# Early expert products in three fp32r passes, their remainders split between VectorE and GpSimd, in a one-layer decoder step

## The reference, cut to what matters

```
def chunk_fn(xc):
    q = (xc @ w_query).astype(jnp.float32).reshape(PEER_CHUNK, PEER_HEADS, D_QUERY)
    s1 = jnp.einsum('chk,nk->chn', q[..., :HALF_Q], k1)
    s2 = jnp.einsum('chk,nk->chn', q[..., HALF_Q:], k2)
    v1, i1 = lax.top_k(s1, PEER_TOPK)
    v2, i2 = lax.top_k(s2, PEER_TOPK)
    cand = (v1[..., :, None] + v2[..., None, :]).reshape(PEER_CHUNK, PEER_HEADS, PEER_TOPK * PEER_TOPK)
    sc, ci = lax.top_k(cand, PEER_TOPK)
    e1 = jnp.take_along_axis(i1, ci // PEER_TOPK, axis=-1)
    e2 = jnp.take_along_axis(i2, ci % PEER_TOPK, axis=-1)
    eid = e1 * N_KEYS + e2
    gate = jax.nn.softmax(sc, axis=-1)
    act = jax.nn.gelu(jnp.einsum('chkd,cd->chk', exp_u[eid], xc, preferred_element_type=jnp.float32))
    out = jnp.einsum('chk,chkd->cd', gate * act, exp_v[eid].astype(jnp.float32))
    return out.astype(xc.dtype)
```

## Time and profile before

| | |
|---|---|
| median of 3 runs | 1710.42 us (1708.64 to 1710.57) |
| the profiled execution, its own time | 1709.66 us |
| its span, first to last instruction | 1707.8 us |
| granted TensorE clock, mean over the span | 0.99 |
| busy: PE, DVE, ACT, POOL | 96%, 77%, 36%, 28% |
| the chain that ended last | PE 78%, DVE 2%, DMA 1%, SP's queue 1% |

### The profile page before, as it was taken

The page is one execution under the profiler, slowest core; times in us unless marked ns, Lnnn a source line. Parts: engine busy times, 40 slices in busy tenths (PEclk is TensorE's granted clock), DMA queues, the critical chain, the costliest instruction groups (busy, mean ns, idle before and its releaser), DMA issues.

```text
span 1707.8 us, 24171 instructions
## 1 busy us (share of the span) xinstructions
PE 1645.9 (96%) x8587; PEld 1373.7 (80%) x8587; DVE 1316.1 (77%) x2697; ACT 618.3 (36%) x1034; POOL 484.3 (28%) x511
## 2 busy tenths in 40 slices
PE   7998988999999999987999999999999999999998
PEld 6777664467777669976999999999999999998886
DVE  5788463247898879976888788888888888889976
ACT  5322452221111158862333333333333333333434
POOL 1000000011223300013444444444444444445420
PEclk9999999999999999998999999999999999999999
DMA  8312813032221127888999999999999999999883
GB/s 283 121 69 71 312 66 118 0 140 75 75 74 50 62 80 221 255 269 298 339 349 353 331 347 356 336 338 357 339 337 352 351 336 342 361 336 356 329 313 140
DMA packets 164427, 411.53 MB, mean 241 GB/s; under 512 B 15503, under 2 KB 76461, under 8 KB 162893
## 3 DMA queue, kind: packets, MB, share of 16 engines
q1 hardware_dynamic: 118229, 242.20, 41.2%
q0 software_dynamic: 46080, 167.79, 26.6%
HBM read 375.34 MB, written 33.24 MB: 239 GB/s over the span
## 4 chain that ended last, share of the span: by engine, by line
PE 78%; DVE 2%; DMA 1%; SPq 1%; ACT 1%; issue 0%; DVEq 0%; ACTq 0%
PE bank L1471 30%; PE bank L1423 25%; PE bank L1410 7%; PE bank L1362 7%; PE bank L1340 3%; PE bank L1452 3%; PE bank L1399 1%; DVE placed L1934 1%; DMA u<-in_uT 1%; SPq L1285 1%; DMA gates_kept<-staged 1%; DVE hot_b L1927 0%; DVE here L1930 0%; DVE h_low L1911 0%; PE bank L1332 0%; ACT qh L1525 0%
## 5 line engine op out<-in xcount | busy, mean ns | idle before, releaser
L1471 PE MATMUL bank<-v_parts,p_high 128*128 128x512 f32 x1404 | 434.7, 391 | 2.4 <-DVE p_low L1911 2.4
L1679 POOL DMA_INDIRECT rows<-in_u_rows,row_u x160 | 198.2, 1239 | 399.5 <-DVE dots L1967 219.9
L1471 PEld LDWEIGHTS bank<-v_parts,p_high 128*128 128x128 f32 x1404 | 262.4, 188 | 51.5 <-issue 3.5
L1423 PE MATMUL bank<-h_high,u_high 128*128 128x384 f32 x832 | 282.7, 340 | 10.6 <-DVE u_low L1911 9.9
L1423 PE MATMUL bank<-h_low,u_high 128*128 128x384 f32 x832 | 283.0, 340 | 0.0
L1679 POOL DMA_INDIRECT rows<-in_v,row_u x160 | 212.9, 1331 | 239.4 <-DVE y L1977 170.5
L1423 PE MATMUL bank<-h_high,u_low 128*128 128x384 f32 x832 | 278.7, 335 | 0.0
L1471 PE MATMUL bank<-v_parts,p_low 128*128 128x512 f32 x702 | 273.6, 390 | 0.0
L1911 DVE TENSOR_TENSOR u_low<-u,u_high 128x1024 fp32r<-128x1024 f32 x115 | 140.8, 1224 | 146.7 <-ACT u_high L1560 146.4
L1596 ACT CAST p_high<-gel 128x384 fp32r<-128x384 f32 x128 | 65.8, 514 | 380.6 <-DVE gel L1955 363.5
L1423 PEld LDWEIGHTS bank<-h_high,u_high 128*128 128x128 f32 x832 | 157.0, 189 | 14.8 <-DVE u_low L1911 10.4
(11 more groups left out here) (235 smaller groups left out, 2440.2 us busy)
## 6 DMA issues: line engine op xcount, KB each, us to landing
vv<-in_v SPq DMA_DIRECT2D x117, 512.0 KB, 5.4
u<-in_uT SPq DMA_DIRECT2D x104, 512.0 KB
gate<-gates_kept SPq DMA_DIRECT2D x30, 768.0 KB, 8.3
gates_kept<-staged SPq DMA_DIRECT2D x11, 2048.0 KB, 9.7
early<-in_uT SPq DMA_DIRECT2D x24, 512.0 KB, 3.6
w_in_sb<-in_w_in SPq DMA_DIRECT2D x9, 1024.0 KB, 8.6
wq<-in_w_q SPq DMA_DIRECT2D x16, 512.0 KB, 3.7
ckT<-in_ckT SPq DMA_DIRECT2D x4, 1536.0 KB, 14.5
```

Source lines behind the costliest of these rows:

```text
L1423: ins = pe.matmul(a_ps[par][:, 0:DT], x[:, par, k], y, start=(k == 0 and n == 0), stop=(k == KT - 1 and n == 2))
L1471: ins = pe.matmul(y_ps[2 * (i - 1) + half][:], x[:, b, of], y[:, part], start=(t == 0 and n == 0), stop=(t == NK - 1 and n == 2))
L1679: nc.gpsimd.indirect_dma_start(rows[:, r % ROW_BUFS], None, table, bass.IndirectOffsetOnAxis(ap=row_u[:, s_:s_ + 1], axis=0)).then_inc(fet ...
```

## The change: what it does

1. The 24 early blocks are computed by `activate` too, with three fp32r products instead of one in fp32. `activate_early`, the buffer `early` and its four places are gone; early blocks go through the two places of `u`.
2. ACT rounds them: the two blocks of a head behind the first and the second half of its query copies, the nine others of the last run each behind a gelu. The remainders of blocks 0 to 14 are taken by DVE at the beginning of a head, those of blocks 15 to 23 by POOL: five of them each behind the sums of one tile of head 7, one behind the last, three behind `pick(7)`.
3. `h_high` is rounded and `h_low` taken ahead of head 0 (ACT, POOL). `split_h` is gone from DVE.
4. POOL does `pick(n - 1)` ahead of the sums of head n, no longer behind them.
5. In the 16 x 16 tables of `hits`, `pick` and `decode` the keys are innermost now: the comparison reads the position broadcast along the innermost axis, and the sum reads along it without a stride.
6. The load of block 34 stands between the two last stores.
7. Memory: `h2T` and `h_low` have places of their own; `tops`, `ef`, `gsum`, `shift` and `row_f` lie where `xr` and `g2_row` were.

```diff
-EARLY_BUFS = 4
+BY_POOL = sum(min(n, 2) for n in IN_HEADS.values())
 ...
+        late = Region(nc, base.at + TILES * D * 4, x_region.at)
 ...
-            def load_early(q):
-                wait(sp, a_done, q - EARLY_BUFS + 1)
-                sp.dma_start(early[:, q % EARLY_BUFS], d.uT[q]).then_inc(early_in[q % EARLY_BUFS], 16)
             def load_u(q, par):
-                first = q < WHOLE + 2
-                sp.wait_ge(a_done, q - EARLY_BUFS + 1 if first else q - 1)
+                wait(sp, a_done, q - 1)
 ...
-            for half in range(2):
-                store_last(half)
+            store_last(0)
             load_u(EARLY + 2, EARLY % 2)
+            store_last(1)
 ...
             def activate(q, par, halves=(0, 1)):
                 if 0 in halves:
-                    pe.wait_ge(u_split, q - WHOLE + 1)
+                    if q == 0:
+                        pe.wait_ge(h_split, KT)
+                    if q < 2:
+                        pe.wait_ge(h0s_ready, 2)
+                    if q < BY_POOL:
+                        pe.wait_ge(early_split, q + 1)
+                    elif q < WHOLE:
+                        pe.wait_ge(last_split, q - BY_POOL + 1)
+                    else:
+                        pe.wait_ge(u_split, q - WHOLE + 1)
 ...
+                    for q in early_after(n)[half:half + 1]:
+                        round_u(q, q % 2)
 ...
             act.wait_ge(h_taken, 2 * TILES)
+            for k in range(KT):
+                nc.scalar.copy(h_high[:, k], h2T[:, k, P:END]).then_inc(h_rounded, 1)
             for n in range(PH):
                 head(n)
-                for q in early_after(n)[:7]:
+                for z, q in enumerate(early_after(n)[:9]):
                     gelu(q)
-            for k in range(KT):
-                nc.scalar.copy(h_high[:, k], h2T[:, k, P:END]).then_inc(h_rounded, 1)
+                    for q in early_after(n)[z + 2:z + 3]:
+                        round_u(q, q % 2)
             act.wait_ge(shifted, 2)
 ...
+            for k in range(KT):
+                pool.wait_ge(h_rounded, k + 1)
+                nc.gpsimd.tensor_tensor(h_low[:, k], h2T[:, k, P:END], h_high[:, k].bitcast(F32), ALU.subtract
+                                        ).then_inc(h_split, 1)
+            def split_early(q):
+                pool.wait_ge(u_rounded, q + 1)
+                nc.gpsimd.tensor_tensor(u_low[:, q % 2], u[:, q % 2], u_high[:, q % 2].bitcast(F32), ALU.subtract
+                                        ).then_inc(last_split, 1)
             for n in range(PH):
+                if n:
+                    pick(n - 1)
                 for i in range(tiles_of(n)):
                     sums(n, i)
-                if n:
-                    pick(n - 1)
+                    if n == PH - 1:
+                        split_early(early_after(n)[2 + i])
+            split_early(early_after(PH - 1)[2 + TILES])
             pick(PH - 1)
+            for q in early_after(PH - 1)[3 + TILES:]:
+                split_early(q)
 ...
-                        slot = cab[:, hh, half, i].rearrange("p (o j) -> p o j", o=1)
+                        slot = cab[:, hh, half, i].rearrange("p (j o) -> p j o", o=1)
 ...
-                    nc.vector.tensor_reduce(ef[:, half, 0:m, n], hit[:, half, 0:m].rearrange("p i k j -> p i j k"), AX_X,
+                    nc.vector.tensor_reduce(ef[:, half, 0:m, n], hit[:, half, 0:m], AX_X,
 ...
             def head(n):
                 m = tiles_of(n)
+                for q in early_after(n)[:2]:
+                    low(u_low[:, q % 2], u[:, q % 2], u_high[:, q % 2], u_rounded, q + 1).then_inc(early_split, 1)
 ...
-                if n == HOTS:
-                    dve.wait_ge(a_done, WHOLE)
-                    split_h()
```

More of the change, by code:

```diff
@@ L1099, in route @@
         keysT = sb("keysT", [P, 2, NK])
+        h2T = sb("h2T", [P, KT, T])
         qh = sb("qh", [P, 4, T])
@@ L1113, in route @@
         keyf = sb("keyf", [P, 2, 2, TILES, TOPK])
[L1114 to L1118, removed]
+        tops = late("tops", [P, TILES, PH, TOPK])
+        ef = late("ef", [P, 2, TILES, PH, TOPK])
+        gsum = late("gsum", [P, TILES, PH])
+        shift = late("shift", [P, TILES, PH, TOPK])
+        row_f = late("row_f", [P, FETCHED])
         spreads = sb("spreads", [P, PACK, NS])
@@ L1173, in route @@
         u_rounded, u_split = sem("u_rounded"), sem("u_split")
-        early_in = [sem(f"early_in{b}") for b in range(EARLY_BUFS)]
+        early_split, last_split = sem("early_split"), sem("last_split")
         gates_copied = [sem(f"gates_copied{b}") for b in range(2)]
@@ L1249, in _ @@
             sp.wait_ge(scaled, TILES)
-            for q in range(EARLY_BUFS):
-                load_early(q)
+            for q in range(2):
+                load_u(q, q % 2)
             for n in range(PH):
@@ L1556, in whole @@
                                hot_b[:, n % 2].rearrange("p g k t -> p g t k")).then_inc(hot_made, 1)
-            def round_u(q, par):
-                act.wait_ge(u_in[par], 8 * (q - WHOLE - par) + 16)
-                nc.scalar.copy(u_high[:, par], u[:, par]).then_inc(u_rounded, 1)
-            for q in early_after(PH - 1)[7:-1]:
+            for z, q in enumerate(early_after(PH - 1)[9:-1], 9):
                 gelu(q)
+                for q in early_after(PH - 1)[z + 2:z + 3]:
+                    round_u(q, q % 2)
             whole(0)
@@ L1656, in pick @@
                     for i in range(tiles_of(n)):
-                        key = keyf[:, hh, half, i].rearrange("p (k o) -> p k o", o=1)
+                        key = keyf[:, hh, half, i].rearrange("p (o k) -> p o k", o=1)
                         ins = nc.gpsimd.tensor_tensor(hit[:, half, i], hit[:, half, i],
@@ L1738, in _, with low @@
                 nc.vector.tensor_tensor(h0s[:, half], banks[6 + n][:], g2_row[:, half], ALU.mult).then_inc(h0s_ready, 1)
+            def low(part, whole, high, rounded, value):
+                dve.wait_ge(rounded, value)
+                return nc.vector.tensor_tensor(part, whole, high.bitcast(F32), ALU.subtract)
             def search(n, i):
@@ L1907, in _ @@
             counts = spread(count[:].rearrange("p (o k) t -> p o k t", o=1), [P, TB // 2, NK, 2])
-            def low(part, whole, high, rounded, value):
-                dve.wait_ge(rounded, value)
-                return nc.vector.tensor_tensor(part, whole, high.bitcast(F32), ALU.subtract)
-            def split_h():
-                for k in range(KT):
-                    low(h_low[:, k, P:END], h2T[:, k, P:END], h_high[:, k], h_rounded, k + 1).then_inc(h_split, 1)
             def split_u(q, par):
-                low(u_low[:, par], u[:, par], u_high[:, par], u_rounded, q - WHOLE + 1).then_inc(u_split, 1)
+                low(u_low[:, par], u[:, par], u_high[:, par], u_rounded, q + 1).then_inc(u_split, 1)
             for n in range(BATCHES):
-                if n == HOTS:
-                    dve.wait_ge(a_done, WHOLE)
-                    split_h()
                 if n % (GB // TB) == 2 and n // (GB // TB) in range(1, IN_GATES + 2):
```

35 lines of the change are left out of this document (10 added, 25 removed).

## The result

The changed kernel takes 1720.95 us (median of 4 runs, 1719.27 to 1723.20) against 1710.49 (1708.64 to 1712.12): a ratio of 1.0062, 95% interval 1.0050 to 1.0075. It is 0.6% slower. The forecast was faster, 1703.8, and its range ended at 1711. The profiled execution took 1719.27 us, its span is 1717.2; before it was 1709.66 and 1707.8. So the ledger has to explain 9.4 us of span.

The account below looks back on a forecast made before the run. PE was taken to bound the heads and the steady stage. Terms -12.1 + 8.5 + 5.0 - 2.0 - 6.0 = -6.6 us gave 1703.1 for the profiled execution, a median of 1703.8 us, range 1696.5 to 1711.

Parts of the forecast that it names:

- Heads: Heads 0 to 7: fp32r blocks shorten PE's period from 28.64 to 26.77 us, -12.1 us in all.
- Last run: Blocks 13 to 23: waits for loads, remainders and gates make it 66.5 us instead of 57.96, +8.5, before clock losses.
- that term: PE's clock falling behind gaps in the last run: 3.0 us for the long hole, 2.0 for four others, +5.0.
- POOL's rate: POOL's remainder of 1024 elements: 1.97 us, extrapolated from operations of 56 and 256 elements, bounds 1.6 to 2.5.
- last run at half clock: Rival: blocks from 15 on at 1.2 GHz, about 24 us lost, 1722.8 us; decided at 81.5 us; chance 0.08.
- Start of the gates: After the last run: DVE's remainder of h is gone, so the gates start earlier, -2.0 us.
- Load of block 34: Turn into the steady stage: queued behind one store, not two, the load lands earlier, -6.0 us.

Follow-up runs that it names:

- e6: Changed kernel with POOL's pick behind the sums of a head again, as before; layout and all else kept: 1725.78 us, ratio 1.0090.
- e12: Changed kernel with blocks 13 to 23 as plain fp32 products and the slots innermost again in `hit`: 1697.44 us, ratio 0.9927.
- e5: Changed kernel with the slots innermost again in `hit`, as before the change; all else kept: 1718.21 us, ratio 1.0046.
- e2: Kernel before the change with only the load of block 34 put between the two last stores: 1710.35 us, ratio 0.9999.
- e7: Changed kernel, blocks 13 to 23 plain fp32, loads of u 34, u 35 and v of step 2 between the last store's halves: 1692.44 us, ratio 0.9897.
- e16: e7 plus blocks 13 and 14 as fp32r (1690.43 us), with `h_low` in rows of 544 instead of 384, as before the change: 1688.67 us, ratio 0.9878.

## Why the prediction was wrong

The forecast was a gain, with a chance of 0.08 for slower, and the kernel got slower: two terms were wrong, the last run and the load of block 34.

**Heads: right.** Forecast -12.1, measured -11.4; the heads themselves gave 12.1, and 0.7 is a later start of the first (348.83 for 348.14), which in the profiles of the experiments varies between 347.8 and 350.7. Period 26.68 against 26.77, two blocks 8.52 against 8.40. On DVE the sum takes 1.21 us (I had 1.38 at most). The comparison takes 0.42 undisturbed, just what I took (the mean of 0.44 has some in it that wait for POOL); one starts every 0.34 us instead of 0.20. The casts fell from 0.59 to 0.19, as the move of the pick had suggested, and e6 shows it: without that move heads 4 and 5 are DVE's. In the changed kernel they are at the limit, with periods of 27.02 and 26.82 us. e12 shows that even the old layout fits in.

**Last run: this step failed, by its size.** Forecast 66.5 + 5.0 = 71.5 us; it took 79.8. The mechanism stood in the forecast, gap by gap. By the stretches of PE's products (pairs from block 13 on: 8.61, 10.19, 10.16, 11.22 us; block 21 4.46; the last two 10.42) the 11 blocks took 55.1 us where full clock gives 46. So that term was 9 us, not 5. Against 4.20 us a block the pairs behind the first three gaps lost 1.8, 1.8 and 2.8 us, where I had 2.0 for all gaps, and the two blocks behind the long hole 2.0, where I had 3.0. Not all of it is the clock: the first pair lost 0.2 us and block 21, behind the fourth gap, 0.3 at a granted clock of 1.00, so a start after a wait costs about that by itself, and the clock some 8. The gaps in front of blocks 15, 17, 19 and 21 are 3.11, 3.09, 5.70 and 3.02 us, the hole 8.95 and `turn_slots` 0.9, together 24.8 where I had 20.3. Of these 4.5 us 0.6 in each of three gaps comes mostly from POOL's 2.35 us for a remainder (I took 1.97), and 2.6 from the remainder of block 19; the gap in front of block 21 was 0.6 shorter than forecast and the hole 0.6 longer.

That remainder is the mechanism that I missed. POOL starts it at 591.11. DVE is at its comparisons until 594.10:

```profile
590.67 3.43 DVE L1830 TENSOR_TENSOR hit<-cab,place 128x256 bf16<-128x256 bf16 x10
```

and POOL is done at 596.31, 2.2 us after the last of them, where a whole remainder takes 2.35. The same in the heads: DVE's comparisons run from 440.27, its remainder to 444.17, and POOL's first product ends 0.53 us later.

```profile
441.77 2.93 POOL L1650 TENSOR_TENSOR hit<-hit,keyf 128x256 bf16<-128x256 bf16 x1 [7.53 <-DVE hit L1830]
```

In all six picks of heads 1 to 6 that product ends 0.53 to 0.55 us after DVE's last two-input instruction, whether it took 2.9 or 4.4 us. So there POOL doesn't run slower; it stands still until the run of them ends. By the Trainium skill (SBUF — State Buffer, "Who interferes with whom") "A DVE instruction with two SBUF inputs contends with a GpSimd instruction that reads SBUF", and the one that comes second is blocked. The trace agrees (2.93 us against 0.67), and so do e5 (2.34) and e6 (0.67, picks begun at other times). It doesn't always wait for the whole run, though. In the first pick of head 0 POOL begins in the same way, inside a run of comparisons, and the two take turns, DVE's comparisons at 0.89 us and POOL's products at 0.85; so they do in `pick(7)` of e6. What decides between the two no run shows.

```profile
L1650 POOL TENSOR_TENSOR hit<-hit,keyf x4: 789/850/854, 389.0 to 391.3; 128x256 bf16<-128x256 bf16 x4
```

The change put POOL's first product right beside DVE's longest such run, so that a wait threatens there could have been read from the order beforehand. The page of the Trainium skill that I weighed for POOL's rate (GPSIMD Engine Reference, "3.1 Elementwise — side-by-side cycle accounting") was right as well: the estimate from its 2.6 cycles, with the launch seen here, was 2.4 us, and the remainder takes 2.35 undisturbed. The slope from operations of 56 and 256 elements was a bad basis.

**The rival "last run at half clock"** named 81.5 us as its point of decision. The run ended 1.7 us short of it. It had 0.08. That the time, 1720.95, lies beside its 1722.8 is chance: it wanted half clock in every block from 15 on and 24 us lost by it, and the loss was 9, since part of each pair and all of block 21 ran at full rate. The rest of the way came from longer waits (4.5), the load of block 34 (5.0) and the steady stage (1.9), none of which it had.

**Start of the gates: right**, -1.9 against -2.0.

**Load of block 34: failed.** Forecast -6.0, measured -1.0, and e2 gives 0 on the median (0.9 in its trace). Block 34 did come earlier: 784.28 - 764.32 = 19.96 us after block 32 and not 26.94. The prediction said "The second store and the loads of v behind it come about 2 us later; block 35 then lands just when PE asks for it". The second store landed at 787.45, 23.1 us after block 32 began, where both had landed 20.5 us after it before, and block 35 waited for it by way of v and ACT's queue. I had followed u of 35 to its landing, but not the rounding behind v of step 2. That is also where e7 found the 5 us.

**What was not forecast at all:** 1.9 us in the steady stage, by the layout of `h_low` (e16).

The sum: 0.7 ahead of the heads, 8.3 in the last run, 0.1, 5.0 and 1.9 make the 16 us between -6.6 and +9.4.

## What to carry to other kernels

A cheaper form of a step that needs a longer chain (load, round, split) pays where the chain is hidden, in the heads, and not where the same few buffers are turned over without pause; there one more buffer for the first link brought 14 us and plain fp32 as much. Follow each wait that you remove to the next consumer on every engine's queue, since a transfer or an Exp queued behind the wrong neighbour cost 9 us here and hid a gain of 5. When an edit moves GpSimd's work, look at what VectorE does at that time: a GpSimd instruction that begins beside its two-input instructions can wait for a whole run of them, and VectorE's short operations can take three times as long beside GpSimd's.

## What the runs showed of the hardware

- A GpSimd instruction of 0.67 us took up to 4.4 us when it began in a run of VectorE's two-input instructions. In other such runs the two engines took turns at 0.85 and 0.89 us an instruction (head 0 of the changed kernel; `pick(7)` of e6, where none of 68 took over 0.9). What decides is open.
- VectorE's one-input operations on 64 numbers (`bits`) took 0.62 us when the pick ran beside them (e6) and 0.19 when it didn't (changed kernel).
- GpSimd takes 2.35 us for 1024 fp32 elements of a two-input operation, VectorE 1.22.
- Behind gaps of 3.1 us between pairs of 24-product blocks the pair lost 1.8 us each, behind one of 5.7 us 2.8; the granted clock read 0.72 and 0.59 in the blocks behind two of them. Behind a fourth gap, of 3.0 us, it read 1.00, and the block lost 0.3 us (third row):

```profile
580.50:586.50 6.00, 6.00 (x25) 6.00 (x26) 2.70 (x16) 1.05 (x1) 3.46 (x7) 0.72 0.01 3
596.40:603.40 7.00, 7.00 (x25) 7.00 (x26) 1.49 (x1) 0.00 (x0) 7.00 (x9) 0.59 0.00 0
610.60:615.00 4.40, 4.40 (x25) 4.37 (x26) 0.00 (x0) 1.05 (x1) 2.40 (x1) 1.00 0.01 4
```

- With rows of 544 instead of 384 numbers in `h_low` 24 products take 4.197 us and not 4.186, but the 18 of the other kind, which don't read it, 4.090 and not 4.121. Over 96 steps that is 1.9 us. Why is open.
